# A block of attention, gated MLP and dilated attention on one core: the first projected chunk by halves of its modulation, and small loads behind the large ones

## The chip, the cores and the metric

The kernel runs on one core of a Trainium2 chip. The metric is the device time of one execution in microseconds. Five engines matter: TensorE (PE, matrix products and transposes), VectorE (DVE), ScalarE (ACT), GpSimd (POOL), and SyncE (SP), which only issues DMA transfers. Each engine runs its own instructions in program order and waits on semaphores for the others.

## The reference, cut to what matters

Two blocks follow each other on a sequence of 256 rows (width 1024) with a context of 256 rows. The first block has two layers of three kinds of attention; the second has a gated MLP and a dilated attention. Only the very start of the first layer is touched by the change:

```python
for l in range(DEPTH):
    sh, sc, gt = jnp.split(jax.nn.silu(c) @ w_ada[l] + b_ada[l], 3, axis=-1)
    sh_c, sc_c, gt_c = jnp.split(jax.nn.silu(c_ctx) @ w_ada[l] + b_ada[l], 3, axis=-1)
    h = rms_norm(x, norm_g[l]) * (1 + sc[:, None]) + sh[:, None]
    hc = rms_norm(ctx, norm_g[l]) * (1 + sc_c) + sh_c
    qa, ka, va, ga, qb, kb, vb, gb, qn, kn, vn, gn = split_proj(h @ w_in[l])
    ...
```

So nothing can be projected before a shift `sh` and a scale `sc` exist. Each has 1024 entries, and both come out of a product with `w_ada`. A product of `h` with `w_in` sums over those 1024 entries. The entries 0 to 511 of shift and scale are all that the first half of that sum needs.

## The kernel before, in words

**The data.** There are four tiles of 128 rows: tiles 0 and 1 are `x`, tiles 2 and 3 are `ctx`. `w_in` (1024 x 3584) is read in seven chunks of 512 columns; a chunk is four pieces, and a piece is 256 rows by 512 columns (512 KB). A piece lands in one of three buffers (`raw`, `RAW = 3`). ScalarE rounds it to `w_hi` and VectorE takes the rest, `w_lo` (`split_until`, four slots, `SPLIT = 4`). A product of a 128-wide slice of `h` with a piece is three matmuls (lines 665 to 667): high with low, low with high, high with high. A chunk is therefore 4 tiles x 8 slices x 3 = 96 matmuls.

**Modulation.** The first 2048 columns of `w_ada` come in four groups j = 0 to 3 of 512 columns and four pieces each (512 KB a piece): j = 0 and 1 are the shift, j = 2 and 3 the scale. `ada_row(j)` multiplies them on TensorE (line 604), `ada_keep_row(j)` copies the row out on VectorE, `ada_columns(j)` turns it into columns (line 612), and `ada_keep` adds the bias and, at j = 3, makes `a_scale` (line 1570).

**Normalising.** ScalarE sums squares of a tile (`square`, line 982), GpSimd makes the reciprocal root (`norm`, `power`, lines 1396 to 1403), VectorE multiplies (`normalise`, line 1583), TensorE transposes (`norm_turns`, line 640). Then the eight slices of the tile are scaled and shifted: slices 0 to 3 on VectorE (line 1596), slices 4 to 7 on ScalarE (line 998). ScalarE rounds to `h_hi` (line 1006) and VectorE subtracts to `h_lo` (line 1605).

**The order in the first chunk.** TensorE goes tile by tile: all 24 products of tile 0 with the transposes of tile 1 ahead of the last 6, then tile 1, and so on. All four groups of `w_ada` are done before the first of them.

**The queues.** SP issues, in this order: the small rows, groups 0 and 1 of `w_ada`, `x`, groups 2 and 3, three pieces of `w_in`, `ctx`, and then a piece each time a buffer of `raw` comes free. GpSimd issues 24 small loads at its start: tables for the rotation (`base_tab`), a mask, 14 gains and 8 lambdas, all but the first two broadcast to 128 partitions. VectorE needs gains and lambdas (lines 1842 to 1854); what it makes of them (`q_gains`) lets GpSimd make the rotation tables (`make_tabs(0)`, 24 operations), ahead of everything that GpSimd does for the heads of chunk 0.

**Behind the first chunk.** While TensorE works on chunk 1, the heads of chunk 0 are processed: ScalarE copies them out of PSUM (line 1061) and squares them (line 1078), VectorE sums (line 1673), GpSimd takes the root (lines 1396 and 1398), VectorE scales (line 1681), GpSimd and VectorE rotate (lines 480, 1699, 1704), TensorE transposes (line 685). TensorE takes the PSUM bank of chunk 0's tile 0 for chunk 1, so it waits for the first copy.

Of the kernel before, what the change touches and what calls it, by code (L numbers as in the profile page):

```python
# [77 lines left out]
SPLIT = 4  # L78

# [132 lines left out]
def first_then_second_block(nc, a, out, known):  # L212
# [11 lines left out]
    with ExitStack() as ctx:  # L224
# [47 lines left out]
        pick = region(17664, (2,))  # L272

# [26 lines left out]
        vt = [st(2048 + 1024 * i, 1024) for i in range(2)]  # L300
        junk = st(4096, 512)
# [81 lines left out]
        def freed(use):  # L383
# [4 lines left out]
            if kind == "norm":  # L388
                _, ph, tt, half = use
                return (scaled_v if half == 0 else scaled_a).seen((ph, tt))  # L390
# [25 lines left out]
            return y_made.seen(("dil", rest[0]))  # L416

# [133 lines left out]
        def _(sp):  # L551
# [6 lines left out]
            for p in ada_pieces(0, range(2)):  # L558
                sp.dma_start(ada_first[:, p[1], p[2], :, :], weight_source(p)).then_inc(*ada_landed[p].at(p))
            sp.dma_start(x[:, 0:2, :], a["x"][0].rearrange("(t p) d -> p t d", p=P)).then_inc(*start_loads["x"].at(0))  # L560
            for p in ada_pieces(0, (2, 3)):
                sp.dma_start(ada_first[:, p[1], p[2], :, :], weight_source(p)).then_inc(*ada_landed[p].at(p))  # L562
            for n, p in enumerate(PIECES):
# [8 lines left out]
                if n == 2:  # L572
                    sp.dma_start(x[:, 2:4, :], a["ctx"][0].rearrange("(t p) d -> p t d", p=P)).then_inc(*start_loads["ctx"].at(0))
# [19 lines left out]
        def _(pe):  # L593
            ring = [0]

            def ada_row(j):

                bank = take(pe, SCORE_BANKS[j % 2], "ada_row", j)
# [8 lines left out]
            def ada_columns(j):  # L607

                bank = take(pe, j, "ada", "ada0", j)
                pe.wait_ge(*ada_row_made.seen(j))  # L610
                for i in range(4):
                    mm = pe.matmul(bank[:, 2 * i:2 * i + 2], ada_rows[j % 2][:, i * P:(i + 1) * P], pick[:, :], start=(i == 0), stop=(i == 3))
# [20 lines left out]
            def norm_turns(ph, tt):  # L633
                turned.add((ph, tt))
                pe.wait_ge(*normed.seen((ph, tt)))
                for half in range(2):
# [4 lines left out]
                    mm.then_inc(*tpose.at((ph, tt, half)))  # L641

# [45 lines left out]
            def project(ph, between=None, after_piece=None):  # L688
                tts = tiles_of(ph)
                pairs = PROJ[ph][1] // 2  # L690
                for c in range(PROJ[ph][0]):
                    pieces = [(ph, c, pair) for pair in range(pairs)]
                    if c == 0 and pairs <= SPLIT:

                        normed_first = ph in ("in0", "in1", "gin", "din")
# [272 lines left out]
        def _(act):  # L968
# [17 lines left out]
            def norm_tile(ph, tt):  # L986
# [6 lines left out]
                if bias and tt == 0:  # L993
                    act.wait_ge(*ada_scale_made.seen(ph))
# [215 lines left out]
            norm_tile("in0", 0)  # L1210
            split_until(SPLIT)
            act.wait_ge(*start_loads["ctx"].seen(0))
            for tt in CTX_TILES:
                for half in range(2):
                    square("in0", tt, half)
                norm_tile("in0", tt - 1)
            norm_tile("in0", 3)
# [118 lines left out]
        def _(pool):  # L1336
# [6 lines left out]
            half = sm(POWER)  # L1343
            pool.dma_start(base_tab[:, :, :, :], a["rope_1"].rearrange("(t p) a d -> p t a d", p=P)).then_inc(*start_loads["tab"].at(0))
# [48 lines left out]

            def power(out_ap, in_ap, n, scale, eps, done, key):
# [667 lines left out]
```

## Time and profile before

| | us |
|---|---|
| median of 3 runs | 1298.64 (1297.81 to 1301.27) |
| profiled execution, device time | 1296.14 |
| its span, first to last instruction | 1294.4 |
| TensorE busy | 1150.7 (89% of the span) |
| VectorE, ScalarE, GpSimd busy | 727.3, 601.9, 250.4 |
| mean granted TensorE clock | 0.952 of full speed |

The span is what the trace covers; 1.74 us of the device time lie outside it. A busy time counts an engine's instructions while they run, and says nothing of which engine the others wait for. Times in the trace count from the span's start.

### The profile page before, as it was taken

The numbers are of one execution on the slowest core, as the hardware profiler recorded it, in microseconds if no ns is written. First come the engines' busy times: TensorE is split into PE (matmuls) and PEld (weight loads), VectorE is DVE, ScalarE is ACT, GpSimd is POOL, SyncE is SP. The second block draws the span as 40 slices with busy tenths as digits, with TensorE's granted clock in tenths as the row PEclk, the third lists the DMA queues.
The fourth block names the chain that finished last, engine by engine and source line by source line (L and its number), as shares of the span: only waits on it lengthen the run. The fifth ranks groups of instructions, "written<-read, shape, count | busy, mean of one in ns | idle before, by whom it ended". The sixth has DMA issues, their size and how long they took to land.

```text
span 1294.4 us, 16688 instructions
## 1 busy us (share of the span) xinstructions
PE 1150.7 (89%) x5877; PEld 910.5 (70%) x5877; DVE 727.3 (56%) x1320; ACT 601.9 (47%) x1174; POOL 250.4 (19%) x324
## 2 busy tenths in 40 slices
PE   4787879899987977989989798998889999999987
PEld 0475557677675866668867686887668888888875
DVE  0448677786763554464444656565465655565543
ACT  0443335444662353454464553444444445445553
POOL 4146060326004104112300204000012211121100
PEclk9798889898997999889989999998999999999999
DMA  8626344333203123213110664553446565434301
GB/s 232 230 89 198 104 136 131 113 115 84 96 2 102 66 82 113 65 53 95 66 49 26 235 217 145 179 177 128 136 155 187 179 185 172 126 118 117 129 1 49
DMA packets 79001, 157.92 MB, mean 122 GB/s; under 512 B 5760, under 2 KB 6056, under 8 KB 78664
## 3 DMA queue, kind: packets, MB, share of 16 engines
q1 hardware_dynamic: 75592, 147.41, 36.2%
q0 software_dynamic: 3328, 9.46, 2.9%
q8 instruction: 48, 0.79, 0.2%
q14 instruction: 33, 0.27, 0.1%
HBM read 153.73 MB, written 3.11 MB: 121 GB/s over the span
## 4 chain that ended last, share of the span: by engine, by line
PE 69%; DVE 10%; ACT 8%; issue 5%; POOL 4%; SPq 2%; DMA 2%; ACTq 0%; POOLq 0%; DVEq 0%
PE bank L665 16%; PE bank L667 16%; PE bank L666 16%; PE bank L803 5%; PE bank L778 3%; PE bank L788 3%; PE bank L878 2%; POOL small L1398 2%; ACT w_hi L977 2%; DVE w_lo L1537 2%; DVE work L1557 2%; PE bank L851 2%; SPq L562 2%; PE bank L863 2%; PE bank L685 1%
## 5 line engine op out<-in xcount | busy, mean ns | idle before, releaser
L665 PE MATMUL bank<-w_lo,h_hi 128*128 128x512 f32 (+1 forms) x1152 | 461.5, 401 | 33.5 <-DVE h_lo L1605 16.7
L666 PE MATMUL bank<-w_hi,h_lo 128*128 128x512 f32 (+1 forms) x1152 | 446.6, 388 | 0.0
L667 PE MATMUL bank<-w_hi,h_hi 128*128 128x512 f32 (+1 forms) x1152 | 446.5, 388 | 0.0
L1537 DVE TENSOR_TENSOR w_lo<-raw,w_hi 128x1024 fp32r<-128x1024 f32 x224 | 285.9, 1282 | 280.9 <-ACT w_hi L977 279.4
L977 ACT ACTIVATE w_hi<-raw 128x1024 fp32r<-128x1024 f32 x224 | 235.8, 1057 | 294.1 <-PE bank L667 249.9
L665 PEld LDWEIGHTS bank<-w_lo,h_hi 128*128 128x128 f32 x1152 | 222.5, 193 | 84.0 <-issue 38.9
L667 PEld LDWEIGHTS bank<-w_hi,h_hi 128*128 128x128 f32 x1152 | 221.6, 192 | 44.9
L666 PEld LDWEIGHTS bank<-w_hi,h_lo 128*128 128x128 f32 x1152 | 223.0, 194 | 40.0 <-issue 0.2
L803 PE MATMUL bank<-work,stage 128*128 128x128 f32 x640 | 94.8, 291 | 1.5 <-ACT stage L1164 1.3
L1155 ACT ACTIVATE stage<-bank,small 128x512 f32<-128x512 f32 (+1 forms) x96 | 56.9, 596 | 71.1 <-DVE small L1752 71.0
L803 PEld LDWEIGHTS bank<-work,stage 128*128 128x128 f32 x640 | 85.2, 204 | 3.3 <-ACT stage L1164 2.7
L1525 POOL TENSOR_TENSOR stage<-stage 128x512 f32<-128x512 f32 x24 | 42.3, 1785 | 218.0 <-DVE stage L480 218.0
L1164 ACT ACTIVATE stage<-bank 128x512 f32<-128x512 f32 (+1 forms) x96 | 50.4, 525 | 72.4 <-PE bank L788 72.1
L788 PEld LDWEIGHTS bank<-ident,stage 128*128 128x128 f32 x320 | 36.8, 147 | 64.8 <-issue 47.6
L788 PE MATMUL bank<-ident,stage 128*128 128x128 f32 x320 | 56.5, 293 | 26.4 <-DVE work L1577 8.0
L778 PE MATMUL bank<-work 64*128 64x512 f32 (+3 forms) x240 | 68.1, 605 | 12.7 <-ACT stage L1155 12.7
L1398 POOL TENSOR_TENSOR small<-small 128x1 f32<-128x1 f32 (+4 forms) x56 | 74.0, 1321 | 4.7
L1396 POOL TENSOR_SCALAR small<-small 128x1 f32<-128x1 f32 (+4 forms) x56 | 17.6, 314 | 283.6 <-DVE small L1673 238.5
L1557 DVE SCALAR_TENSOR_TENSOR work<-raw,cvec,work 128x512 f32<-128x512 f32 x98 | 71.3, 777 | 0.5 <-DMA raw<-in_w_ada_dram 0.3
L1752 DVE TENSOR_REDUCE small<-bank 128x1 f32<-128x512 f32 (+1 forms) x96 | 53.1, 572 | 13.8 <-PE bank L778 13.7
L1787 DVE SCALAR_TENSOR_TENSOR work<-bank,small,work 128x64 f32<-128x64 f32 x96 | 27.0, 281 | 48.4 <-PE bank L803 34.6
L1094 ACT ACTIVATE work<-bank 128x512 f32<-128x512 f32 (+2 forms) x56 | 29.9, 534 | 35.0 <-PE bank L685 35.0
(166 smaller groups left out, 1102.3 us busy)
## 6 DMA issues: line engine op xcount, KB each, us to landing
raw<-in_b_w_in_dram SPq DMA_DIRECT2D x80, 512.0 KB, 3.6
raw<-in_w_in_dram SPq DMA_DIRECT2D x56, 512.0 KB, 3.7
raw<-in_a_w_in_dram SPq DMA_DIRECT2D x48, 512.0 KB, 4.0
raw<-in_w_ada_dram SPq DMA_DIRECT2D x32, 512.0 KB, 3.7
work<-in_w_ada_dram SPq DMA_DIRECT2D x16, 512.0 KB, 13.9
raw<-in_w_out_dram SPq DMA_DIRECT2D x16, 512.0 KB, 3.5
raw<-in_a_w_out_dram SPq DMA_DIRECT2D x16, 512.0 KB, 3.5
raw<-in_b_w_out_dram SPq DMA_DIRECT2D x8, 512.0 KB, 3.5
```

Source lines behind the costliest of these rows:

```text
L665: pe.matmul(bank, hT(h_hi, ph, kt, tt), w_lo[:, s, k, lo:lo + w], start=first, stop=False)
L666: pe.matmul(bank, hT(h_lo, ph, kt, tt), w_hi[:, s, k, lo:lo + w], start=False, stop=False)
L667: mm = pe.matmul(bank, hT(h_hi, ph, kt, tt), w_hi[:, s, k, lo:lo + w], start=False, stop=last)
L778: mm = pe.matmul(bank[:, k0:512], qkT[base:base + d, tq, qt * P:(qt + 1) * P], qkT[base:base + d, tk, k0:512], start=True, stop=True)
L788: mm = pe.transpose(bank[:, j * P:(j + 1) * P], probs[prob_slot(layer, u, 0)][:, j * P:(j + 1) * P], ident[:, :])
L803: mm = pe.matmul(bank[:, 0:P], pT[i % 2][:, j * P:(j + 1) * P], vals[:, j, vcol:vcol + P], start=(j == kt0), stop=(j == 3))
L977: act.activation(w_hi[:, i % SPLIT, :, :], raw[:, PIECE_AT[p] % RAW, :, :], ACT.Copy) \
L1155: act.activation(probs[slot][:, k0:512], bank[:, k0:512], ACT.Exp, bias=nm_col(u, m), accum_out=zc[0]).then_inc(*exps.at((layer, n)))
L1398: pool.tensor_tensor(out_ap, out_ap, half.broadcast_to([P, n]), ALU.pow).then_inc(*done.at(key))
L1537: dve.tensor_tensor(w_lo[:, i % SPLIT, :, :], raw[:, PIECE_AT[p] % RAW, :, :], w_hi[:, i % SPLIT, :, :].bitcast(F32), ALU.subtract).then_i ...
L1557: dve.scalar_tensor_tensor(to, w, c, to, ALU.mult, ALU.add).then_inc(*ada_vector.at((*p, k, who)))
L1752: dve.tensor_reduce(nm_col(u, m), bank[:, k0:512], AX, ALU.max, negate=True).then_inc(*row_max.at((u, m)))
```

## The change

It touches only what stands ahead of chunk 1 of layer 0.

- SP issues group 0 of `w_ada`, `x`, `ctx`, group 2, two pieces of `w_in`, then groups 1 and 3, then the other pieces.
- `a_scale` is made in two halves, from group 2 and from group 3.
- TensorE takes the first chunk in two halves of the sum. In each it goes through the four tiles with two pieces; the transposes of a tile's half stand two tiles ahead; groups 1 and 3 are multiplied between the tiles.
- The scaling is shared by tile: VectorE scales the even tiles, ScalarE the odd ones, four slices at a time, into buffers of their own (`first_vt`). The normalised tiles have four buffers (`first_xn`) in place of two.
- GpSimd makes the reciprocal roots first and issues its 24 small loads when group 3 has landed. VectorE does its gains and lambdas after the whole first chunk.

```diff
+FIRST_ROWS = (0, 2, 1, 3)
+
...
         vt = [st(2048 + 1024 * i, 1024) for i in range(2)]
+        first_xn = [st(1024 * i, 1024) for i in range(4)]
...
-            for p in ada_pieces(0, range(2)):
+            for p in ada_pieces(0, (0,)):
                 sp.dma_start(ada_first[:, p[1], p[2], :, :], weight_source(p)).then_inc(*ada_landed[p].at(p))
             sp.dma_start(x[:, 0:2, :], a["x"][0].rearrange("(t p) d -> p t d", p=P)).then_inc(*start_loads["x"].at(0))
-            for p in ada_pieces(0, (2, 3)):
+            sp.dma_start(x[:, 2:4, :], a["ctx"][0].rearrange("(t p) d -> p t d", p=P)).then_inc(*start_loads["ctx"].at(0))
+            for p in ada_pieces(0, (2,)):
                 sp.dma_start(ada_first[:, p[1], p[2], :, :], weight_source(p)).then_inc(*ada_landed[p].at(p))
...
                 sp.dma_start(raw[:, n % RAW, :, :], weight_source(p)).then_inc(*landed[n % RAW].at(p))
-                if n == 2:
-                    sp.dma_start(x[:, 2:4, :], a["ctx"][0].rearrange("(t p) d -> p t d", p=P)).then_inc(*start_loads["ctx"].at(0))
+                if n == 1:
+                    for q in ada_pieces(0, (1, 3)):
+                        sp.dma_start(ada_first[:, q[1], q[2], :, :], weight_source(q)).then_inc(*ada_landed[q].at(q))
...
+
+            def first_turn(tt, half):
+                pe.wait_ge(*normed.seen(("in0", tt)))
+                bank = take(pe, 6 + tt % 2, "norm", "in0", tt, half)
+                for i in range(4):
+                    kt = half * 4 + i
+                    mm = pe.transpose(bank[:, i * P:(i + 1) * P], first_xn[tt][:, kt * P:(kt + 1) * P], ident[:, :])
+                mm.then_inc(*tpose.at(("in0", tt, half)))
+
+            def first_chunk(pieces):
+
+                for half in range(2):
+                    for tt in ALL_TILES:
+                        if half == 0 and tt == 3:
+                            ada_columns(1)
+                            ada_row(3)
+                        for p in pieces[2 * half:2 * half + 2]:
+                            if tt == 0:
+                                weights(p)
+                            if p[2] % 2 and tt + 2 in ALL_TILES:
+                                first_turn(tt + 2, half)
+                            for k in range(2):
+                                product("in0", 0, p, k, tt)
+                            if (p[2], tt) == (0, 3):
+                                first_turn(0, 1)
+                                first_turn(1, 1)
+                                ada_columns(3)
+                        if half == 0 and tt == 1:
+                            ada_row(1)
...
+                    if c == 0 and ph == "in0":
+                        first_chunk(pieces)
+                        continue
...
             ada_row(0)
-            ada_row(1)
             ada_columns(0)
             ada_row(2)
-            ada_columns(1)
-            norm_turns("in0", 0)
-            ada_row(3)
+            first_turn(0, 0)
             ada_columns(2)
-            ada_columns(3)
+            first_turn(1, 0)
...
-            norm_tile("in0", 0)
-            split_until(SPLIT)
...
+            for half in range(2):
+                split_until(2 * half + 1)
+                first_scale(1, half)
+                first_h_hi(0, half)
+                split_until(2 * half + 2)
+                first_h_hi(1, half)
+                first_h_hi(2, half)
+                first_scale(3, half)
+                first_h_hi(3, half)
+            split_until(6)
             act.wait_ge(*setup_v.seen("lambda_sums"))
             act.activation(sm(LAM_EXP, 4), sm(LAM_SUM, 4), ACT.Exp).then_inc(*setup_a.at("lambda_exp"))
...
+            norm("in0")
+            pool.wait_ge(*ada_landed[("ada0", 3, 3)].seen(("ada0", 3, 3)))
             pool.dma_start(base_tab[:, :, :, :], a["rope_1"].rearrange("(t p) a d -> p t a d", p=P)).then_inc(*start_loads["tab"].at(0))
...
-                if j == 3:
-                    g = cols[:, 16 + 8 * layer:24 + 8 * layer].unsqueeze(2).broadcast_to([P, KT, 2])
+                if j in (2, 3):
+                    k = 4 * (j - 2)
+                    g = cols[:, 16 + 8 * layer + k:20 + 8 * layer + k].unsqueeze(2).broadcast_to([P, 4, 2])
                     dve.wait_ge(*ada_kept.seen((name, j)))
-                    dve.scalar_tensor_tensor(a_scale[:, :, :], ada_cols[:, 8:16, :], 1.0, g, ALU.add, ALU.mult) \
-                        .then_inc(*ada_scale_made.at(f"in{layer}"))
+                    dve.scalar_tensor_tensor(a_scale[:, k:k + 4, :], ada_cols[:, 8 + k:12 + k, :], 1.0, g, ALU.add, ALU.mult) \
+                        .then_inc(*ada_scale_made.at((f"in{layer}", j - 2)))
...
             ada_keep_row(0)
-            ada_keep_row(1)
             ada_keep("ada0", 0)
-            for tt in X_TILES:
+            for tt in (0, 1, 2):
                 normalise("in0", tt)
             ada_keep_row(2)
-            ada_keep("ada0", 1)
+            normalise("in0", 3)
+            ada_keep("ada0", 2)
+            for half in range(2):
+                first_scale(0, half)
+                split_until(2 * half + 1)
+                first_h_lo(0, half)
+                split_until(2 * half + 2)
+                first_h_lo(1, half)
+                first_scale(2, half)
+                first_h_lo(2, half)
+                if half == 0:
+                    ada_keep_row(1)
+                first_h_lo(3, half)
+                if half == 0:
+                    ada_keep("ada0", 1)
+                    ada_keep_row(3)
+                    ada_keep("ada0", 3)
+            split_until(6)
             dve.wait_ge(*start_loads["lambdas"].seen((3, 1)))
...
-            ada_keep_row(3)
-            ada_keep("ada0", 2)
-            ada_keep("ada0", 3)
-            norm_tile("in0", 0)
-            split_until(SPLIT)
-            for tt in ALL_TILES[1:]:
-                if tt - 1 in X_TILES:
-                    normalise("in0", tt + 1)
-                norm_tile("in0", tt)
```

SP, the queue of loads, at the start of the program, before (`work<-in_w_ada` is `w_ada`, `raw<-in_w_in` is `w_in`, x8 is eight pieces):

```order
L559 DMA work<-in_w_ada_dram 128x2x512 x8
L560 DMA x<-in_x_dram 128x2x1024
L562 DMA work<-in_w_ada_dram 128x2x512 x8
L571 DMA raw<-in_w_in_dram 128x2x512 x3
L573 DMA x<-in_ctx_dram 128x2x1024
L571 DMA raw<-in_w_in_dram 128x2x512 x6
```

and after:

```order
L569 DMA work<-in_w_ada_dram 128x2x512 x4
L570 DMA x<-in_x_dram 128x2x1024
L571 DMA x<-in_ctx_dram 128x2x1024
L573 DMA work<-in_w_ada_dram 128x2x512 x4
L582 DMA raw<-in_w_in_dram 128x2x512 x2
L585 DMA work<-in_w_ada_dram 128x2x512 x8
L582 DMA raw<-in_w_in_dram 128x2x512 x7
```

`ctx` has moved ahead of everything but group 0 and `x`, and two pieces of `w_in` stand ahead of groups 1 and 3.

TensorE from the first product of `w_ada` to the first piece of chunk 0, before (with the number of the PSUM bank; 32x512 are products of `w_ada`, 128x2 its columns, `ident` marks transposes):

```order
L604 MATMUL bank4<-work 32x512 x8
L604 MATMUL bank5<-work 32x512 x8
L612 MATMUL bank0<-work 128x2 x4
L604 MATMUL bank4<-work 32x512 x8
L612 MATMUL bank1<-work 128x2 x4
L640 MATMUL bank6<-ident,stage 128x128 x4
L640 MATMUL bank7<-ident,stage 128x128 x4
L604 MATMUL bank5<-work 32x512 x8
L612 MATMUL bank2<-work 128x2 x4
L612 MATMUL bank3<-work 128x2 x4
L665 MATMUL bank0<-w_lo,h_hi 128x512
```

and after:

```order
L616 MATMUL bank4<-work 32x512 x8
L625 MATMUL bank4<-work 128x2 x4
L616 MATMUL bank5<-work 32x512 x8
L661 MATMUL bank6<-ident,stage 128x128 x4
L625 MATMUL bank5<-work 128x2 x4
L661 MATMUL bank7<-ident,stage 128x128 x4
L707 MATMUL bank0<-w_lo,h_hi 128x512
...
L709 MATMUL bank0<-w_hi,h_hi 128x512
L661 MATMUL bank6<-ident,stage 128x128 x4
L707 MATMUL bank0<-w_lo,h_hi 128x512
```

Two groups of `w_ada` stand ahead of the first matmul of the chunk where four stood, and the first transposes of tile 2 (bank 6) stand behind six matmuls.

VectorE, from the scaling of the first tile to the lambdas and the gains, after the change, in the second half of the sum (`w_lo` is the rest of a piece, `h_lo` the rest of a tile):

```order
L1912 TENSOR_SCALAR work<-bank,a_scale,ada_cols 128x128 x4
L1605 TENSOR_TENSOR w_lo<-raw,w_hi 128x1024
L1919 TENSOR_TENSOR h_lo<-work,h_hi 128x4x128
L1605 TENSOR_TENSOR w_lo<-raw,w_hi 128x1024
L1919 TENSOR_TENSOR h_lo<-work,h_hi 128x4x128
L1912 TENSOR_SCALAR work<-bank,a_scale,ada_cols 128x128 x4
L1919 TENSOR_TENSOR h_lo<-work,h_hi 128x4x128 x2
L1605 TENSOR_TENSOR w_lo<-raw,w_hi 128x1024 x2
L1948 ISA stage,small<-stage 128x32
L1948 ISA small 128x1
...
L1956 TENSOR_SCALAR gains<-gains 128x32
L1956 TENSOR_SCALAR gains<-gains 128x64 x3
```

Before, the lambdas and the gains (here from `stage,small<-stage` on) stood ahead of the first scaling:

```order
L1565 TENSOR_TENSOR ada_cols<-bank,cols 128x8
L1845 ISA stage,small<-stage 128x32
L1845 ISA small 128x1
...
L1853 TENSOR_SCALAR gains<-gains 128x32
L1853 TENSOR_SCALAR gains<-gains 128x64 x3
...
L1825 COPY work<-bank 128x512
L1565 TENSOR_TENSOR ada_cols<-bank,cols 128x8 x2
L1570 SCALAR_TENSOR_TENSOR a_scale<-ada_cols,cols 128x16
L1596 TENSOR_SCALAR stage<-bank,a_scale,ada_cols 128x128 x4
L1605 TENSOR_TENSOR h_lo<-stage,h_hi 128x4x128 x2
L1537 TENSOR_TENSOR w_lo<-raw,w_hi 128x1024 x4
```

They have moved from ahead of the chunk to behind its last `h_lo` and behind two pieces of chunk 1.

## Rows read from the trace of the kernel before

**Rows 1.** The page of the whole run: span, and the chain by engine.

```profile
span 1294.4 us, 16688 instructions
...
PE 69%; DVE 10%; ACT 8%; issue 5%; POOL 4%; SPq 2%; DMA 2%; ACTq 0%; POOLq 0%; DVEq 0%
...
```

**Rows 2.** TensorE in order of time: start, length, line, tiles, count, [idle before].

```profile
...
39.65 1.05 PE L612 MATMUL bank<-work 128*128 128x2 f32 x8
...
41.57 2.11 PE L604 MATMUL bank<-work 128*32 128x512 f32 x12
43.96 1.05 PE L604 MATMUL bank<-work 128*32 128x512 f32 x4 [0.29 <-DMA work<-in_w_ada_dram]
...
52.38 0.76 PE L665 MATMUL bank<-w_lo,h_hi 128*128 128x512 f32 x1 [5.48 <-DVE w_lo L1537]
...
59.39 1.03 PE L640 MATMUL bank<-ident,stage 128*128 128x128 f32 x8
...
79.86 0.47 PE L665 MATMUL bank<-w_lo,h_hi 128*128 128x512 f32 x1 [1.56 <-DVE h_lo L1605]
...
86.01 0.47 PE L665 MATMUL bank<-w_lo,h_hi 128*128 128x512 f32 x1 [0.43 <-ACT stage L1061]
...
108.94 1.11 PE L685 MATMUL bank<-ident,stage 128*128 128x128 f32 x4 [5.03 <-DVE stage L1704]
...
```

**Rows 3.** DMA queues, 8 to 28 us.

```profile
...
q1 hardware_dynamic: 2317, 4.77, 68.4%
q0 software_dynamic: 680, 0.51, 31.1%
...
```

**Rows 4.** DMA queues, 28 to 44 us.

```profile
...
q1 hardware_dynamic: 2832, 5.86, 100.7%
...
```

**Rows 5.** GpSimd in order of time.

```profile
...
13.84 1.12 POOL L1354 DMA_DIRECT2D stage<-in_lambda_k_dram  x2
...
65.58 0.25 POOL L1418 TENSOR_TENSOR tabs<-gains,base_tab 128x32 f32<-128x32 f32 x1
65.79 0.69 POOL L1420 TENSOR_TENSOR tabs<-base_tab,gains 128x16 f32<-128x16 f32 x1
...
70.93 0.75 POOL L1421 TENSOR_TENSOR tabs<-base_tab,gains 128x32 f32<-128x32 f32 x1
88.65 0.21 POOL L1396 TENSOR_SCALAR small<-small 128x16 f32<-128x16 f32 x1 [16.97 <-DVE small L1673]
...
```

**Rows 6.** DMA queues, 0 to 43.96 us: packets, MB, share of 16 engines.

```profile
...
q1 hardware_dynamic: 5565, 11.16, 73.3%
...
```

**Rows 7.** DMA queues, 0 to 8 us.

```profile
...
q1 hardware_dynamic: 418, 0.54, 30.6%
q0 software_dynamic: 104, 0.20, 22.0%
...
```

**Rows 8.** VectorE in order of time, the same columns.

```profile
...
41.27 0.87 DVE L1853 TENSOR_SCALAR gains<-gains 128x32 f32<-128x32 f32 x8
...
46.93 0.17 DVE L1565 TENSOR_TENSOR ada_cols<-bank,cols 128x8 f32<-128x8 f32 x1 [0.73 <-PE bank L612]
...
47.41 1.37 DVE L1596 TENSOR_SCALAR stage<-bank,a_scale,ada_cols 128x128 f32<-128x128 f32 x4
49.48 1.29 DVE L1605 TENSOR_TENSOR h_lo<-stage,h_hi 128x512 fp32r<-128x512 f32 x2 [0.70 <-ACT h_hi L1006]
50.94 3.50 DVE L1537 TENSOR_TENSOR w_lo<-raw,w_hi 128x1024 fp32r<-128x1024 f32 x3 [0.17 <-ACT w_hi L977]
...
```

**Rows 9.** ScalarE in order of time.

```profile
...
47.43 1.50 ACT L998 ACTIVATE stage<-bank,ada_cols,a_scale 128x128 f32<-128x128 f32 x4 [10.96 <-DVE a_scale L1570]
...
84.32 1.06 ACT L977 ACTIVATE w_hi<-raw 128x1024 fp32r<-128x1024 f32 x1 [0.30 <-PE bank L667]
...
```

**Rows 10.** One stretch: us, busy (x count) of each engine, TensorE clock, DMA.

```profile
...
52.40:85.42 33.02, 28.17 (x120) 22.18 (x120) 15.78 (x30) 16.46 (x34) 7.95 (x30) 0.91 0.22 66
...
```

**Rows 11.** Transfers issued up to 150 us: KB each, us to landing.

```profile
...
stage<-in_lambda_k_dram POOLq DMA_DIRECT2D x4, 16.0 KB, 9.8
...
```

More of the change, by code:

```diff
@@ L272, in first_then_second_block @@
         pick = region(17664, (2,))
+        first_vt = [[region(17672 + 1024 * half + 512 * i, (512,)) for i in range(2)] for half in range(2)]
         gv = region(0, (2, GMLP))
@@ L416, in freed, with first_scaled @@
             return y_made.seen(("dil", rest[0]))
+        def first_scaled(tt, half):
+            return (scaled_a if tt % 2 else scaled_v).seen(("in0", tt, half))
         def freed_by(ph, c, tt):
@@ L1343, in _, with power, norm @@
             half = sm(POWER)
+            def power(out_ap, in_ap, n, scale, eps, done, key):
+                pool.tensor_scalar(out_ap, in_ap, scale, eps, ALU.mult, ALU.add).then_inc(*means.at((done.name, key)))
+                pool.wait_ge(*means.seen((done.name, key)))
+                pool.tensor_tensor(out_ap, out_ap, half.broadcast_to([P, n]), ALU.pow).then_inc(*done.at(key))
+            def norm(ph, tiles=None):
+                for tt in tiles or tiles_of(ph):
+                    pool.wait_ge(*squares.seen((ph, tt, 1)))
+                    pool.tensor_tensor(sm(RS + tt), sm(SS + 2 * tt), sm(SS + 2 * tt + 1), ALU.add).then_inc(*rstd.at((ph, tt, "sum")))
+                    pool.wait_ge(*rstd.seen((ph, tt, "sum")))
+                    power(sm(RS + tt), sm(RS + tt), 1, 1.0 / D, EPS, rstd, (ph, tt))
+            norm("in0")
+            pool.wait_ge(*ada_landed[("ada0", 3, 3)].seen(("ada0", 3, 3)))
             pool.dma_start(base_tab[:, :, :, :], a["rope_1"].rearrange("(t p) a d -> p t a d", p=P)).then_inc(*start_loads["tab"].at(0))
@@ L1392, in mask_bias @@
                 ins.then_inc(*bias_masked.at(layer))
-            def power(out_ap, in_ap, n, scale, eps, done, key):
-                pool.tensor_scalar(out_ap, in_ap, scale, eps, ALU.mult, ALU.add).then_inc(*means.at((done.name, key)))
-                pool.wait_ge(*means.seen((done.name, key)))
-                pool.tensor_tensor(out_ap, out_ap, half.broadcast_to([P, n]), ALU.pow).then_inc(*done.at(key))
-            def norm(ph, tiles=None):
-                for tt in tiles or tiles_of(ph):
-                    pool.wait_ge(*squares.seen((ph, tt, 1)))
-                    pool.tensor_tensor(sm(RS + tt), sm(SS + 2 * tt), sm(SS + 2 * tt + 1), ALU.add).then_inc(*rstd.at((ph, tt, "sum")))
-                    pool.wait_ge(*rstd.seen((ph, tt, "sum")))
-                    power(sm(RS + tt), sm(RS + tt), 1, 1.0 / D, EPS, rstd, (ph, tt))
             def make_tabs(layer):
```

60 lines of the change are left out of this document (45 added, 15 removed).

## The prediction

> **What bounds the kernel now.** I read the page first: TensorE holds 69% of the chain that ended last [rows 1]. From chunk 1 on, the change alters no instruction, so what it can give is how much earlier the work behind chunk 0 starts, and whether that lead survives. Then I read the start engine by engine. The last quarter of group 3 of `w_ada` lands at 43.96 and the first matmul of chunk 0 starts at 52.38, after 5.48 us of waiting for a `w_lo` [rows 2]. So the start is bound by transfers, and then by a chain on VectorE. Inside chunk 0 TensorE waits some 1.6 us for each of tiles 1 to 3 (the row at 79.86 is the last of three) and leaves it at 85.6, where it waits 0.43 us for a copy [rows 2]. Next the windows of the queues. In 8 to 28 us the hardware queue (SP's) is busy for 68.4% and the software queue (GpSimd's small loads) for 31.1%, though these move 0.51 MB against 4.77 [rows 3]; later the hardware queue is busy all the time [rows 4]. Behind chunk 0 the path is the chain of the heads. GpSimd's first root starts at 88.65, 3.1 us after the chunk's end, and TensorE waits 5.03 us for the result of this chain at 108.94 [rows 2, 5]. So the number to predict is not the end of chunk 0 but the start of that root: what it gains, the kernel gains.
>
> **Step 1, the transfers.** A piece is 0.52 MB, a group of `w_ada` 2.10, `x` and `ctx` 1.05 each. Before, 9.49 MB stood in SP's order up to the end of group 3, and the queue had moved 11.16 when it landed [rows 6]; 1.67 MB of later transfers had gone in between. After, 6.34 MB stand up to the end of group 2, the first that chunk 0 needs: 8.0 with the same excess. The rate: 4.77 MB in 68.4% of 20 us is 349 GB/s of busy queue, 5.86 in 16 us is 366 [rows 3, 4]. I take 355, nearer the early one. In the first 8 us the queue moved 0.54 MB at 30.6% [rows 7]; with the 22.0% of the small loads given to it, 0.93. So group 2 has landed at 8 + 7.07 / 0.355 = 28.0. Bounds: with half the excess and 366 GB/s it is 25.0; with 0.54 MB at 8 us and 349 GB/s, 29.4; if the small loads' share isn't given back at all, the hardware queue needs its old time: 3.16 MB less than at 43.96, at 366 GB/s 8.6 us earlier, 35.3.
>
> **Step 2, up to the first matmul.** From the landing at 43.96 to the first scaling at 47.41 took 3.45, of which 0.90 were a second wait and addition (46.93) that is gone [rows 8]: 2.55. Then a scaling of 1.37, a `w_lo` of 1.2 (a third of 3.50), an `h_lo` of 0.65 (half of 1.29) [rows 8], 0.2 to start. That is 6.0 in place of 8.4: the first matmul at 34.0. The piece of `w_in` lands some 1.5 us behind the group, and ScalarE's rounding of 1.06 [rows 9] hides in the 2.55 and the scaling.
>
> **Step 3, the first half of the sum.** In the last tile before, 24 matmuls took 5.72 (79.86 to 85.58), 0.238 each. The first 18 took 7.0 (52.38 to 59.39) where 18 x 0.238 is 4.3: 2.7 lost, and the granted clock of the whole stretch is 0.91 [rows 2, 10]. The half has 48 matmuls (11.4), that loss with a transpose in it (3.0), four half transposes of 0.5 (eight in 1.03: 2.0), groups 1 and 3 (12 instructions in 2.11, so 16 in 2.8: 5.6) and their columns (1.05 each: 2.1) [rows 2]. Sum 24.1, end 58.1. Nothing else waits in it: tiles 1 to 3 are scaled two tiles ahead, and group 3 has landed at 8 + 12.3 / 0.355 = 42.7 (11.6 MB in order and 1.67 of excess), where it is wanted at about 50. The three waits of 1.6 are gone, 4.8 us; the 7.7 of groups 1 and 3 have come in. That much of the earlier start is only borrowed.
>
> **Step 4, the second half.** Its scale comes from the columns of group 3, which stand six matmuls ahead of the half's end: 56.7. Addition and `a_scale` 0.5, scaling 1.37, `w_lo` 1.2 (it is queued ahead of `h_lo`), `h_lo` 0.65, start 0.2: 60.6. So a new wait of 2.5 us stands here. Then 48 matmuls and two half transposes, 12.4: chunk 0 ends at 73.0, 12.6 earlier than before.
>
> **Step 5, what has moved behind the chunk.** VectorE does lambdas and gains behind the last `h_lo` and two `w_lo` of chunk 1, and they need ScalarE. Its last scaling waits for the transpose of tile 3, at 65.9, takes 1.50, an `h_hi` 0.55, two `w_hi` 1.06 each [rows 9]: 70.1. VectorE ends the second `w_lo` at 71.3, the lambdas at 71.8, the gains (0.87) at 72.7 [rows 8]. Only then can GpSimd make its tables: 65.58 to 71.68, 6.1 us [rows 5]. They were done 17 us before the first root and cost nothing; now they end at 78.8. Without them the root would start at 73.0 + 3.1 = 76.1, or 77.2 with one more `w_hi` ahead of the copies. So they are late next, by 1.6 to 2.7 us. The root starts at 78.8 in place of 88.65: **9.85 us gained**. The 24 small loads start at 42.7, take 0.56 each to issue (13.84, two in 1.12), so until 56.1, and the last kind lands 9.8 later [rows 5, 11]: 65.9, 5.4 us ahead of the 71.3 at which VectorE asks. Their cover is those 5.4 us; after that each microsecond costs one.
>
> In the tables one operation of GpSimd took 0.69 and another 0.75 where its like took 0.25, each beside an operation of VectorE [rows 5]. The Trainium skill, SBUF — State Buffer, section Who interferes with whom, says that the two engines share a pair of ports under an exclusive lock, held for a whole instruction, and the page adds that descriptors of GpSimd's transfers can't be written meanwhile. By the row a clash costs 0.5; by the page, beside a `w_lo`, up to 1.2, which would put the tables at 79.5 to 80 and the gain at 9. It speaks against the new place of the small loads, and that is the fourth rival.
>
> **The sum.** The profiled execution took 1296.14 and would take 1286.3. The median of the runs, 1298.64, lies 2.5 above that execution; against it the forecast is 1298.64 - 9.85 = **1288.8**.
>
> **The rivals.**
> - *The queue is quicker still.* For: nothing stops it later, 366 GB/s. Against: the excess was there in full. Group 2 at 25.0, 3 us more: 1285.8.
> - *Half of the small loads' share comes back.* Their packets may have overlapped with others. Group 2 at about 32: gain 6, 1292.7.
> - *None of it comes back*, group 2 at 35.3: only the new order counts. Gain 2.55, 1296.1, no change that can be told. For: shares of busy time don't say that one queue kept the other waiting. Against: 349 GB/s of busy queue in 8 to 28 us and 366 later [rows 3, 4]; it moved its bytes at the same rate whenever it was on.
> - *The small loads land late.* VectorE is busy 15.78 of 33.02 us in chunk 0, 48% [rows 10]. If GpSimd can't issue beside it, 13.4 us become 25.8, they land at 78.3, 7 us late: 1295.8. Before, they were issued while VectorE was idle, so the trace doesn't exclude it.
> - *Slower: the clock stays at 1.2 GHz through chunk 0.* Short bursts between waits could hold it there. The 78 matmuls behind the first 18 then cost up to 0.238 more, 18.6 us: 1307.4. It ends on the other side from 58 slow ones on (13.8 us). Against: before, waits of 1.6 did not lower it [rows 2, 10], and the work is denser now.
>
> **How the numbers follow.** Forecast (1286.5 to 1291) 0.43, quicker queue 0.15, half share 0.17, none 0.11, late small loads 0.08, slow clock 0.06. From these 1284.5 to 1295.5 leaves out no more than 2 in 10. This kernel's measurement tells 0.3%, 3.9 us, from nothing. Over that lie the first three and a little of the late loads: faster 0.79. Same is none of the share and the rest of the late loads, 0.15. Slower 0.06.
>
> **What would show it.** First matmul of chunk 0 at 34 (31 to 41 by the cases); no software queue before 42; one wait of about 2.5 us in the chunk's middle and none for tiles 1 to 3; the chunk's end near 73; tables ending near 79 and the first root at once behind them; the wait for the second transpose of heads still about 5 us. I am wrong if the software queue's absence leaves the hardware queue below 95% busy in 8 to 28 us, if VectorE waits for the lambdas, or if the lead at the first root isn't the lead at the kernel's end.

## The result, and the profile after

| | before | changed |
|---|---|---|
| median of runs, same chip, us | 1299.95 (1297.81 to 1301.53) | 1284.28 (1282.64 to 1284.82) |
| ratio | | 0.9877, interval 0.9856 to 0.9899 |
| profiled execution, its span | 1296.14, 1294.4 | 1282.64, 1280.9 |

The change gives 15.7 us where 9.85 were forecast. The median lies 4.5 us below the forecast of 1288.8 and 0.2 below its range of 1284.5 to 1295.5. Direction and mechanism were right, the size was not.

The page after, whole run: busy time by engine, and the chain that ended last.

```profile
PE 1150.2 (90%) x5877; PEld 915.1 (71%) x5877; DVE 726.2 (57%) x1322; ACT 602.4 (47%) x1174; POOL 250.8 (20%) x324
...
PE 71%; DVE 11%; ACT 7%; POOL 5%; issue 4%; DMA 2%; SPq 0%; ACTq 0%; POOLq 0%; DVEq 0%
```

Each engine has within 1.1 us the work that it had in the table of before; the shares of the chain are those of [rows 1] within two points. So the time has to come from when things start. The queues after, 8 to 28 us:

```profile
DMA packets 3542, 7.88 MB, mean 394 GB/s; under 512 B 208, under 2 KB 208, under 8 KB 3542
...
q1 hardware_dynamic: 3542, 7.88, 104.5%
```

and from the start to 21.7 us, when group 2 has landed:

```profile
q1 hardware_dynamic: 3076, 6.71, 84.0%
```

The hardware queue now fills all 20 us and moves 7.88 MB in place of 4.77 [rows 3]. Up to the landing of group 2 it moved 6.71 MB where 6.34 stand in order: an excess of 0.37, not 1.67. TensorE after, in order of time (start, length, line, count, idle before and its releaser):

```profile
17.63 5.11 PE L616 MATMUL bank<-work 128*32 128x512 f32 x16 [3.44 <-DMA work<-in_w_ada_dram]
...
28.41 0.76 PE L707 MATMUL bank<-w_lo,h_hi 128*128 128x512 f32 x1 [3.27 <-DVE h_lo L1919]
...
36.58 1.92 PE L616 MATMUL bank<-work 128*32 128x512 f32 x16
...
42.19 1.92 PE L616 MATMUL bank<-work 128*32 128x512 f32 x16
...
51.14 0.47 PE L707 MATMUL bank<-w_lo,h_hi 128*128 128x512 f32 x1 [2.27 <-DVE h_lo L1919]
...
65.82 0.47 PE L707 MATMUL bank<-w_lo,h_hi 128*128 128x512 f32 x1 [0.97 <-ACT stage L1103]
...
83.07 1.12 PE L727 MATMUL bank<-ident,stage 128*128 128x128 f32 x4 [3.40 <-DVE stage L1773]
...
91.52 0.66 PE L727 MATMUL bank<-ident,stage 128*128 128x128 f32 x4 [3.48 <-DVE stage L1773]
```

The first matmul of chunk 0 starts at 28.41 in place of 52.38 [rows 2]. There is one wait inside the chunk, at its middle; the chunk ends at 64.85, and the transposes of heads come at 83.07 and 91.52. The latter is the 108.94 of [rows 2], 17.4 us earlier. This **lead** at that one transpose is the measure used for every kernel below. GpSimd after:

```profile
64.95 0.29 POOL L1487 TENSOR_TENSOR tabs<-gains,base_tab 128x32 f32<-128x32 f32 x1 [16.37 <-DVE small L1963]
65.21 0.21 POOL L1489 TENSOR_TENSOR tabs<-base_tab,gains 128x16 f32<-128x16 f32 x1
65.39 1.19 POOL L1490 TENSOR_TENSOR tabs<-base_tab,gains 128x16 f32<-128x16 f32 x1
...
71.21 0.21 POOL L1413 TENSOR_SCALAR small<-small 128x16 f32<-128x16 f32 x1
```

The root at 71.21 has no wait before it: the tables end right ahead of it and hold it back, as forecast. It comes 17.44 earlier than in [rows 5].

**From the lead to the medians.** The two profiled spans differ by 13.5 only. Four us of the lead are lost between the same two matmuls far behind chunk 0. The stretch in the kernel before, then changed (us, busy and count of PE, PEld, DVE, ACT, POOL, then the clock):

```profile
407.90:529.99 122.09, 103.60 (x501) 84.37 (x501) 57.12 (x86) 47.40 (x87) 25.11 (x30) 0.95 0.26 80
```

```profile
391.80:517.97 126.17, 108.40 (x502) 87.72 (x501) 57.11 (x86) 47.41 (x87) 25.02 (x30) 0.91 0.26 77
```

The same instructions take 4.1 us more at a granted clock of 0.91 against 0.95. Is that the change's doing? In a later run that keeps most of the old timing (the small loads first, lead 3.8) the same stretch took 127.46 at 0.90. From the second transpose of heads to the end of the span, the profiled execution of before took 1185.5 us, and the eleven other profiled executions 1188.1 to 1191.2, whether their lead is 3.8 or 22.8. And the profiled execution of before, 1296.14, is quicker than each of the four runs in the table, while the runs of before in the later comparisons go from 1295.12 to 1305.31. So the 0.95 most likely belonged to that execution, and the medians follow the lead, not the difference of these two spans.

### The profile page after: what moved, and what is told of

The parts are those of the page before. It is cut to its first block, busy times and chain, and to the rows that moved or that the text cites. A ratio compares the mean times of both kernels' runs of the same rounds, so it can differ in the third digit from the quotient of the medians.

```text
span 1280.9 us, 16699 instructions
## 1 busy us (share of the span) xinstructions
PE 1150.2 (90%) x5877; PEld 915.1 (71%) x5877; DVE 726.2 (57%) x1322; ACT 602.4 (47%) x1174; POOL 250.8 (20%) x324
## 4 chain that ended last, share of the span: by engine, by line
PE 71%; DVE 11%; ACT 7%; POOL 5%; issue 4%; DMA 2%; SPq 0%; ACTq 0%; POOLq 0%; DVEq 0%
PE bank L707 17%; PE bank L709 16%; PE bank L708 16%; PE bank L848 5%; PE bank L833 3%; PE bank L823 3%; POOL small L1415 2%; DVE w_lo L1605 2%; PE bank L923 2%; ACT w_hi L1019 2%; DVE work L1625 2%; PE bank L896 2%; PE bank L908 1%; PE bank L727 1%; POOL stage L490 1%
## 5 line engine op out<-in xcount | busy, mean ns | idle before, releaser
L1625 DVE SCALAR_TENSOR_TENSOR work<-raw,cvec,work 128x512 f32<-128x512 f32 x98 | 71.2, 777 | 0.5 <-DMA raw<-in_w_ada_dram 0.2
L1821 DVE TENSOR_REDUCE small<-bank 128x1 f32<-128x512 f32 (+1 forms) x96 | 53.2, 573 | 13.5 <-PE bank L823 13.5
```

What stands on the lines that cost most here:

```text
L1625: dve.scalar_tensor_tensor(to, w, c, to, ALU.mult, ALU.add).then_inc(*ada_vector.at((*p, k, who)))
L1821: dve.tensor_reduce(nm_col(u, m), bank[:, k0:512], AX, ALU.max, negate=True).then_inc(*row_max.at((u, m)))
```

## The experiments

All were compared with the kernel before on the same chip. "First" is the first matmul of chunk 0, "lead" is 108.94 less the start of the second transpose of heads.

| kernel | first | lead | median (range) | before | ratio (interval) |
|---|---|---|---|---|---|
| changed, again | 29.25 | 17.8 | 1283.04 (1282.55 to 1285.39) | 1301.89 | 0.9865 (0.9845 to 0.9886) |
| small loads first | 43.16 | 3.8 | 1296.02 (1291.83 to 1297.43) | 1301.89 | 0.9955 (0.9939 to 0.9971) |
| gains in the gap | 29.14 | 21.1 | 1279.36 (1278.05 to 1281.41) | 1301.89 | 0.9835 (0.9814 to 0.9856) |
| group 3 sooner | 28.41 | 18.8 | 1280.95 (1277.38 to 1284.70) | 1301.89 | 0.9845 (0.9819 to 0.9871) |
| before, small loads late | 38.55 | 8.3 | 1290.45 (1290.15 to 1294.67) | 1301.47 | 0.9920 (0.9890 to 0.9950) |
| groups 1, 3 ahead | 37.70 | 7.9 | 1293.05 (1286.87 to 1294.20) | 1301.47 | 0.9920 (0.9889 to 0.9951) |
| both together | 28.75 | 22.8 | 1278.16 (1274.49 to 1279.44) | 1301.47 | 0.9811 (0.9786 to 0.9836) |
| tables alone first | 28.68 | 17.2 | 1284.19 (1281.79 to 1285.30) | 1301.47 | 0.9859 (0.9837 to 0.9882) |
| broadcasts by ScalarE | 38.39 | 8.4 | 1292.45 (1291.48 to 1294.04) | 1300.32 | 0.9945 (0.9923 to 0.9966) |
| lambdas first | 34.42 | 11.8 | 1288.87 (1287.95 to 1289.74) | 1300.32 | 0.9910 (0.9879 to 0.9940) |

In each row the lead is within 2.8 us of the difference of the medians.

### The changed kernel again

No edit; the kernels below are set against it.

> The changed kernel itself once more, beside the others of this call. Both theories: median 1283 to 1285, 15 to 16 us below the kernel before. In the trace the lead over the kernel before is 20 us at chunk 1 and 17.4 at the first root of the heads, and the rest is lost in steps of 0.2 us per matmul where the granted clock of TensorE stands at another level than before; if that loss is chance, it falls in other places in this execution and has another size; if it belongs to the change, it falls in the same places.

It came 18.85 us below before, with a lead of 17.8 (transpose at 91.14). Its second half of chunk 0 took 12.10 at a clock of 1.00, where the first profile has 13.71.

### Small loads first

```diff
             half = sm(POWER)
+            pool.dma_start(base_tab[:, :, :, :], a["rope_1"].rearrange("(t p) a d -> p t a d", p=P)).then_inc(*start_loads["tab"].at(0))
+            pool.dma_start(win_mask[:, :], a["window"]).then_inc(*start_loads["mask"].at(0))
+            for layer in range(2):
...
             norm("in0")
-            pool.wait_ge(*ada_landed[("ada0", 3, 3)].seen(("ada0", 3, 3)))
...
```

> The changed kernel with one edit: GpSimd issues its 24 small loads at its start again. Theory A, the small loads hold back the large ones: group 2 of w_ada lands at 31 to 35 us in place of about 22, the first matmul of chunk 0 at 37 to 41 in place of 28.4, and the time rises by 9 to 13 us. Rival B, the earlier start comes from the order of the large loads alone: the first matmul stays at 28 to 30 and the time within 2 us of the changed kernel. What I forecast, a mere share of busy time given back, lies between: 34 us and 6 us.

TensorE, in order of time:

```profile
31.60 5.88 PE L616 MATMUL bank<-work 128*32 128x512 f32 x16 [6.27 <-DMA work<-in_w_ada_dram]
38.38 1.02 PE L625 MATMUL bank<-work 128*128 128x2 f32 x8 [0.30 <-DVE work L1893]
...
43.16 0.77 PE L707 MATMUL bank<-w_lo,h_hi 128*128 128x512 f32 x1 [3.27 <-DVE h_lo L1917]
```

and its queues, 8 to 28 us:

```profile
q1 hardware_dynamic: 2001, 4.85, 65.4%
q0 software_dynamic: 681, 0.51, 32.4%
```

The place of 24 small loads alone moves the first matmul by 13.9 us against the run above and the median by 13.0. The two rows of the queues are nearly those of [rows 3] again, in a kernel whose order of large loads is the new one. Up to 36.4, about when group 2 has landed, the hardware queue moved 8.47 MB: 2.1 over the 6.34 in order. So the excess that I had kept for the changed kernel belongs to the small loads: with them it is there, without them it is 0.37. I took the overtaking by later transfers for a habit of this queue; it comes and goes with the small loads.

### The kernel before with its small loads late

```diff
             half = sm(POWER)
...
+            norm("in0", (0, 1))
+            pool.wait_ge(*ada_landed[("ada0", 3, 3)].seen(("ada0", 3, 3)))
             pool.dma_start(base_tab[:, :, :, :], a["rope_1"].rearrange("(t p) a d -> p t a d", p=P)).then_inc(*start_loads["tab"].at(0))
...
+            norm("in0", (2, 3))
```

VectorE's lambdas and gains stand behind chunk 0 here too.

> The kernel before with the other half of the change alone: the 24 small loads wait for group 3 of w_ada, and VectorE's lambdas and gains stand behind its first chunk; order of the large loads, of TensorE and of the scaling as before. Putting the small loads first cost the changed kernel 13 us, most of the change. Theory A, the small loads are the main part whatever the order: group 3 lands at 8 + (9.49 + 0.35 - 1.27) / 0.394 = 30 in place of 43.96, the first matmul of chunk 0 at 38 in place of 52.4, and the time falls by 10 to 14 us to 1287 to 1291. Rival: the two parts need each other, since all four groups still stand ahead of the chunk, and the time falls by less than 5.

TensorE's rows, in order of time:

```profile
38.55 0.77 PE L665 MATMUL bank<-w_lo,h_hi 128*128 128x512 f32 x1 [5.49 <-DVE w_lo L1540]
...
47.56 0.47 PE L665 MATMUL bank<-w_lo,h_hi 128*128 128x512 f32 x1 [1.74 <-DVE w_lo L1540]
52.31 0.47 PE L665 MATMUL bank<-w_lo,h_hi 128*128 128x512 f32 x1 [3.13 <-DVE h_lo L1608]
```

The first matmul comes 13.8 us sooner than in [rows 2]: all four groups of `w_ada` are still loaded first, and they simply come sooner. It keeps a lead of 8.3, since the chunk's own waits are back, one of them at 3.13, and the tables are late here as well. So this one move carries 11.0 of 18.9 us, and the rest of the change, the new order of loads and of TensorE's work, adds some 8 to 9 (7.9 by the medians, 9.1 by the lead). Alone, in the run above, the new order gives 5.9 or 3.8: each is worth more with the other, by 5 us of lead and by 2 of the medians, which their ranges can hardly tell apart.

### Groups 1 and 3 ahead of `w_in`

```diff
-            for p in ada_pieces(0, (2,)):
+            for p in ada_pieces(0, (2, 1, 3)):
                 sp.dma_start(ada_first[:, p[1], p[2], :, :], weight_source(p)).then_inc(*ada_landed[p].at(p))
...
-                if n == 1:
-                    for q in ada_pieces(0, (1, 3)):
-                        sp.dma_start(ada_first[:, q[1], q[2], :, :], weight_source(q)).then_inc(*ada_landed[q].at(q))
```

> The changed kernel with groups 1 and 3 of w_ada issued ahead of the first two pieces of w_in, everything else as changed. The first matmul then needs 4.2 MB more. If the start is bound by the bytes ahead of it, at 394 GB/s the first piece of w_in lands 10.6 us later (33.7 in place of 23.1), the first matmul comes at 38 in place of 28.4, but TensorE then finds groups 1 and 3 there, so the time rises by 8 to 10 us. Rival: the queue interleaves its transfers so much that the order matters little, and the first matmul moves by less than 4 us.

The row of TensorE's first product, and the one of ScalarE that it hangs on:

```profile
37.70 0.76 PE L704 MATMUL bank<-w_lo,h_hi 128*128 128x512 f32 x1 [12.60 <-DVE h_lo L1916]
```

```profile
33.86 1.06 ACT L1016 ACTIVATE w_hi<-raw 128x1024 fp32r<-128x1024 f32 x1 [14.25 <-DMA raw<-in_w_in_dram]
```

With 4.2 MB ahead of `w_in`, ScalarE waits 14.25 us for the first piece, and 9.5 of the lead of 17.4 are gone. What is left, 7.9, is no more than the 8.3 of the kernel before with its small loads late. So work by halves is worth nothing here unless SP's order follows it.

### Which small loads, and by which queue

Three kernels divide the same cost. Only the rotation table and the mask first:

```diff
             half = sm(POWER)
+            pool.dma_start(base_tab[:, :, :, :], a["rope_1"].rearrange("(t p) a d -> p t a d", p=P)).then_inc(*start_loads["tab"].at(0))
+            pool.dma_start(win_mask[:, :], a["window"]).then_inc(*start_loads["mask"].at(0))
...
```

> The changed kernel with the two loads that are no broadcasts (rotation tables, 144 KB, and mask, 32 KB) at GpSimd's start again, the 22 broadcasts behind group 3. If the broadcasts are what held the large loads back, the first matmul stays at 28.4 to 29.5 and the time within 1 us of the changed kernel. If any transfer on the software queue costs its share of bytes (0.18 of 0.71 MB), the first matmul comes 3 to 4 us later and the time rises by 3.

Only the eight lambdas first:

```diff
             half = sm(POWER)
+            for i, name in enumerate(("lambda_q1", "lambda_k1", "lambda_q2", "lambda_k2")):
+                for layer in range(2):
+                    pool.dma_start(lam[:, i, layer, :], a[name][layer:layer + 1, :].broadcast_to([P, 32])) \
+                        .then_inc(*start_loads["lambdas"].at((i, layer)))
...
```

> The changed kernel with only the 8 lambdas (16 KB each, 0.13 of the 0.53 MB of broadcasts) at GpSimd's start, the 14 gains and the tables behind group 3. If a broadcast costs by its number (8 of 22, of 14 us), the first matmul comes 5 us later, at 34; if by its bytes, 3.5 us later, at 32; if only the whole crowd does harm, it stays below 30.

All 22 broadcasts first, issued by ScalarE on a hardware queue:

```diff
+                    act.dma_start(gains[:, layer, col:col + n], a[name][layer:layer + 1, :].broadcast_to([P, n])) \
+                        .then_inc(*start_loads["gains"].at((layer, name)))
...
+                    act.dma_start(lam[:, i, layer, :], a[name][layer:layer + 1, :].broadcast_to([P, 32])) \
+                        .then_inc(*start_loads["lambdas"].at((i, layer)))
             act.wait_ge(*setup_v.seen("cols"))
...
```

> The changed kernel with its 22 broadcasts issued at the start again, but from ScalarE, on its hardware queue, in place of GpSimd's software queue (tables and mask behind group 3 as changed). If the reading of one small row 128 times is what held the large loads back, the queue doesn't matter: first matmul at 40 to 43 us and a time 10 to 14 us above the changed kernel. If it was the software queue, the first matmul stays below 32 and the time within 3 us of the changed kernel.

The table and the mask cost nothing that shows: first matmul 28.68, queue as in the changed kernel. Their 0.18 MB were through by 6 us, when the large loads had hardly begun, so no run shows what they would cost beside these. But the hardware queue had moved 1.19 MB by 8 us with them, against 1.27 in the changed kernel and 0.44 with the lambdas' 0.13 MB in their place. The lambdas, read from TensorE and from the queues in 8 to 28 us:

```profile
34.42 0.76 PE L707 MATMUL bank<-w_lo,h_hi 128*128 128x512 f32 x1 [3.27 <-DVE h_lo L1919]
```

```profile
q1 hardware_dynamic: 2901, 6.63, 86.9%
q0 software_dynamic: 173, 0.08, 14.8%
```

Eight transfers of 16 KB move the first matmul by 5.2 to 6.0 us (against 29.25 and 28.41), 0.65 to 0.75 each; the 24 move it by 13.9, 0.63 for each of the 22 broadcasts. By number they would have cost 5.1 (8 of 22), by bytes (0.13 of the broadcasts' 0.52 MB) 3.5. So the cost goes by the number of broadcasts rather than by their bytes, as far as one execution of each kernel tells; the first matmul of the same kernel stood at 28.41 and at 29.25.

With ScalarE as issuer, its rows, TensorE's, and the queues in 8 to 28 us:

```profile
16.23 1.28 ACT L1256 ACT_TABLE_LOAD   x1 [16.23 <-issue]
```

```profile
18.17 3.64 PE L616 MATMUL bank<-work 128*32 128x512 f32 x16 [12.10 <-DVE work L1904]
...
27.33 5.38 PE L616 MATMUL bank<-work 128*32 128x512 f32 x12 [0.93 <-DMA work<-in_w_ada_dram]
```

```profile
q1 hardware_dynamic: 2656, 6.17, 84.3%
q10 hardware_dynamic: 2299, 0.37, 10.2%
```

ScalarE is busy with issuing until 16.2, and TensorE's first product waits for it by way of VectorE. That spoils the comparison in part. But of the products of group 2, which begin at 24.48, those at 27.33 wait for their load. They end at 32.71; in the changed kernel, where the 16 from 17.63 on are the same products, they end at 22.74. So group 2 itself is some 10 us late. The first matmul is 9.1 us late against the repeated run, where the software queue made it 13.9. So about two thirds of the cost stay on a hardware queue. What in a broadcast holds the large loads isn't settled. The Trainium skill, DMA: Bandwidth & Descriptors, section Queues, rings and completion order, says that each DMA engine takes turns between its queues packet by packet; the shares agree in kind (in the run with the small loads first q0 takes 32.4% of the time for 0.51 MB), but no run here separates that from the reading of one row 128 times.

### The gains in VectorE's gap

The lambdas and gains move from behind the chunk to ahead of the last `h_lo`, where VectorE waited 3.56 us for ScalarE.

```diff
                     ada_keep_row(1)
+                else:
+                    q_gains()
                 first_h_lo(3, half)
```

> The changed kernel with VectorE's lambdas and gains moved from behind the first chunk into its idle time ahead of the last h_lo of tile 3 (3.56 us of it at 56.7). If GpSimd's tables hold up the first root of the heads, they now end at about 64, the root starts at 68.4 in place of 71.2, and the time falls by 2.8 us. If the root is held by the copies of ScalarE in any case, it stays at 71 and nothing changes. If the small loads haven't landed by 56.7, VectorE waits and the last h_lo is late.

GpSimd, then TensorE:

```profile
58.57 0.25 POOL L1487 TENSOR_TENSOR tabs<-gains,base_tab 128x32 f32<-128x32 f32 x1 [10.03 <-DVE gains L1934]
...
67.50 0.21 POOL L1413 TENSOR_SCALAR small<-small 128x16 f32<-128x16 f32 x1 [0.36 <-DVE small L1742]
```

```profile
64.85 0.47 PE L707 MATMUL bank<-w_lo,h_hi 128*128 128x512 f32 x1 [0.43 <-ACT stage L1103]
...
79.37 0.66 PE L727 MATMUL bank<-ident,stage 128*128 128x128 f32 x4 [0.64 <-DVE stage L1773]
87.83 1.12 PE L727 MATMUL bank<-ident,stage 128*128 128x128 f32 x4 [5.06 <-DVE stage L1773]
```

The root now waits 0.36 for VectorE's sum, not for the tables; it comes 3.1 us behind the chunk's end (64.42), as before the change. The first transpose's wait falls from 3.39 to 0.64, the lead grows by 3.3 and the median falls by 3.7. This shows that the tables were the next to be late, and what it cost.

### Group 3 sooner, and both together

The product of group 3 follows group 1's, and its columns stand ahead of tile 3, so that the scale of the second half is ready earlier; the `w_lo` of the third piece is made ahead of the second half's scaling.

```diff
                             ada_columns(1)
-                            ada_row(3)
+                            first_turn(0, 1)
+                            first_turn(1, 1)
+                            ada_columns(3)
...
                             ada_row(1)
+                            ada_row(3)
```

> The changed kernel with group 3 of w_ada multiplied beside group 1, its columns and the transposes of tiles 0 and 1 taken ahead of tile 3 in the first half, and the w_lo of the third piece ahead of the scaling of the second half. If the wait of 2.27 us in the middle of chunk 0 is the chain from the columns of group 3, it shrinks to about 1.1, the second half starts at 50.0 in place of 51.1, and chunk 0 and the first root come 1.1 us earlier. Rival: group 3 hasn't landed when TensorE asks for it at 38.5, and the wait only moves ahead of tile 2.

TensorE, in order of time:

```profile
17.62 3.76 PE L616 MATMUL bank<-work 128*32 128x512 f32 x12 [3.52 <-DMA work<-in_w_ada_dram]
21.68 1.05 PE L616 MATMUL bank<-work 128*32 128x512 f32 x4 [0.30 <-DMA work<-in_w_ada_dram]
...
51.34 0.47 PE L706 MATMUL bank<-w_lo,h_hi 128*128 128x512 f32 x1 [1.50 <-DVE h_lo L1918]
```

The middle wait falls from 2.29 to 1.50, not to nothing: the chain of scaling, `w_lo` and `h_lo` then hangs on VectorE's order. The lead grows by 1.0; the median by 2.1, which its range of 7 us can't tell apart. (The 21.68 is where group 2's landing is read: here alone its last quarter has a row of its own, and the load order is the changed kernel's.) Then both edits:

> The changed kernel with two edits that were run one at a time: lambdas and gains in VectorE's idle time ahead of the last h_lo, and group 3 one tile earlier. If the two gains add, the lead at the first transpose of the heads is 22 us (17.8 changed, 21.0 and 18.8 with one edit each) and the median is 1277 to 1279. Rival: with the tables out of the way the copies of ScalarE set the root, which the earlier group 3 moves as well, or the small loads, which have not moved, now land late for VectorE; then it is no better than 1279.4.

TensorE's rows of it:

```profile
50.63 0.47 PE L706 MATMUL bank<-w_lo,h_hi 128*128 128x512 f32 x1 [1.50 <-DVE h_lo L1918]
63.17 0.47 PE L706 MATMUL bank<-w_lo,h_hi 128*128 128x512 f32 x1 [0.43 <-ACT stage L1102]
77.69 0.66 PE L726 MATMUL bank<-ident,stage 128*128 128x128 f32 x4 [0.64 <-DVE stage L1772]
86.14 1.12 PE L726 MATMUL bank<-ident,stage 128*128 128x128 f32 x4 [5.04 <-DVE stage L1772]
```

They show both effects side by side, with a lead of 22.8. The median of 1278.16 is the lowest of all, 23.3 us below before and below the changed kernel too.

## Why the prediction was wrong

**Step 1, the transfers, failed.** It said that group 2 has landed at 28.0. It landed at 21.7, 6.3 us sooner, outside my bounds of 25.0 to 35.3. Three terms of the sum made it up. The excess was put at 1.67 MB and was 0.37: 1.3 / 0.355 = 3.7 us. The rate was put at 355 GB/s and was 394: 5.44 MB behind 8 us take 13.8 in place of 15.3, 1.5 us. By 8 us the queue had moved 1.27 MB, not 0.93: 1.0 us. All three are one mistake: I took the removed small loads to cost their share of busy time and read everything else as the queue's own habit. The run with the small loads first brings all three back with all else as in the change: 0.43 MB by 8 us, 4.85 in the next 20, an excess of 2.1. The trace of before had a better rate to offer. [rows 4] is the hardware queue alone, and its 366 GB/s are a mean over 16 us that begin at 337 (28 to 32). Its last 4 us, 40 to 44, are:

```profile
DMA packets 715, 1.56 MB, mean 390 GB/s; under 512 B 41, under 2 KB 41, under 8 KB 715
```

So my bound of 366 was an average with the recovery in it, and the undisturbed rate stood in the same trace. The Trainium skill, Perfetto Trace Analysis, section Roofline, says that a core alone can pull more than its 358 GB/s share, up to about 435; the trace agrees, with 394 here, and by that page too 366 was no upper bound.

**Step 2** held in its size: 6.7 us from the landing to the first matmul, 6.0 forecast.

**Step 3:** the half took 20.5 us (28.41 to 48.87), not 24.1. Groups 1 and 3 take 1.92 each where I put 2.8, scaled from rows in which the matmuls followed their landing; what is left for the 48 products behind groups (3.7), columns (1.7) and transposes (1.9) is 13.1, with the slow ones at the start, instead of 14.4. None of tiles 1 to 3 waits, as forecast.

**Step 4:** the new wait in the middle was forecast at 2.5 and is 2.27. The second half took 13.71 in the first profile against 12.4 forecast. Ten instructions there, from 52.41 to 55.40, are at a granted clock of 0.50. Of the ten profiled executions that work by halves, six took 12.10 to 12.15 at 1.00, the repeated run among them, and four took 13.69 to 13.71 at 0.88 (the first profile, groups 1 and 3 ahead, tables alone, lambdas first). The same kernel shows both, so it isn't the change's order alone that decides; what does stays open. The forecast had the quicker of the two sizes.

**Step 5** held: the tables take 6.2 us (64.95 to 71.13), end ahead of the root and hold it. The small loads are issued from 35.5 to 48.6, the last kind lands 5.2 later, and VectorE begins its lambdas at 63.48 without a wait. The wait of 5 us that I expected at the second transpose of heads is 3.48; late tables delay the first transpose too, which waits 3.40 where it waited 0.59 before. With the gains in the gap the two waits are 0.64 and 5.06. The operation at 65.39 took 1.19 beside a `w_lo` of VectorE (65.23 to 66.50), its likes 0.21 to 0.23: a clash cost 1.0, where the row of before gave 0.5. The rule that I had weighed, of the Trainium skill, SBUF — State Buffer, section Who interferes with whom, has the loser wait for the whole instruction; the trace agrees with that, at one place.

**The sum.** At the root the forecast had 78.8 and the trace 71.2, 7.6 apart: 6.3 from the landing, less 0.7 in step 2, 3.6 from the half, 0.2 from the middle wait, less 1.3 for the second half, less 0.6 behind the chunk (7.5, the rest is rounding). The median shows 4.5 of this on the first chip. The forecast set out from a median of 1298.64; the repeated medians of before are 1299.95 to 1301.89, so the change is worth 15.7 to 18.9 by the medians and 17.4 to 17.8 by the lead. So a low figure for before hid some 3 us of the miss. By one of my signs of being wrong, the lead at the root was to be the lead at the end; the two spans show 17.4 and 13.5, and the 4 us between them are put down above to the one execution of before.

**The rivals.** That only part of the small loads' share, or none, comes back is ruled out by the run with the small loads first. Late small loads are ruled out by the row at 63.48, with about 10 us to spare; beside VectorE's work GpSimd issued them in 13.1 us, where 13.4 were forecast without it. The slow clock did appear, for some 3 us at the chunk's start and 3 us in its second half, and not through the chunk. The quicker queue was right in kind, and its 25.0 was still 3.3 late.

## What to carry to other kernels

Count the small loads that run beside the first large ones, and above all the broadcasts: here 22 of them, 0.52 MB in all, cost 13.9 us at the first matmul. When a change removes traffic, don't carry the disturbed queue's rate and order over to the new kernel; ask of each what it would be alone, look for a stretch of the old trace in which the queue is alone and has recovered, and let the range reach that far. Compare two traces at one same instruction near the change, since a difference of whole spans also holds each execution's clock, 4 us in this case.

## What the runs showed that I had not expected

- A broadcast of 16 to 32 KB to 128 partitions delays the large loads by 0.63 to 0.75 us each, while a plain table of 144 KB and a mask of 32 KB together cost nothing that shows (28.68 against 28.41 and 29.25), though they were through before most of the large traffic began. Issued by ScalarE on a hardware queue the broadcasts still cost 9.1 us.
- The hardware queue alone moves 394 GB/s over 20 us, at 104.5% by the row's measure.
- With small loads beside it the queue doesn't only slow down: 1.7 to 2.1 MB of later transfers overtake the one that is waited for, against 0.37 without them.
